# A two-layer trunk on one core: a unit's queries projected ahead of its values, and two kinds of weight tiles packed in pairs

## The chip, the cores and the metric

The kernel runs on one core of one Trainium2 chip. The metric is the device time of one execution in microseconds (us). Engines are named as in the profile: PE is TensorE's matrix multiply, PEld its weight load, DVE VectorE, ACT ScalarE, POOL GpSimd, SP SyncE, which only issues transfers. L1941 is line 1941 of the kernel before. In the changed kernel the same lines of the engines' programs stand 19 lines further down (L1941 is L1960 there, L1134 L1153, L2085 L2104).

## The reference

1,024 tokens with 16 meta tokens ahead of them (1,040 in all) pass two layers of width 1,024; each adds its result to the scaled input and normalises.

```python
# layer 0 (even): two groups of heads share one input projection
qa, ka, va, ga, qs, ks, vs, gs = split_cols(x @ w_in, EVEN_SPLITS)
# A: 4 units of differential attention with a distance bias, softmax of two maps
w = p[:, :, 0] - lam * p[:, :, 1];  ya = rms_norm(w @ va) * silu(ga)
# B: 8 heads (4 units of two) of stick-breaking attention, times silu(gs)
# layer 1 (odd): latent attention, 8 heads
cq, ckv, k_pe, g = split_cols(x @ w_in, ODD_SPLITS)
q  = rms_norm(cq, q_norm) @ w_uq      # 128 plain and 64 rotary columns per head
kv = rms_norm(ckv, kv_norm) @ w_ukv   # 128 key and 128 value columns per head
# both: concatenated, gated, one output projection, then
h = layer_norm(ALPHA * h + y, ln_g[i], ln_b[i])
```

## The kernel before

All matrices are fp32 split into a high part in fp32r and a low remainder, and each product is the sum of three (high x high, high x low, low x high). A projection step is named (kind, unit, chunk): kinds q0, k0, v0, g0 are queries, keys, values and gate of a unit of layer 0; kn, vn, qn, qr the keys, values, plain queries and rotary queries of a head of layer 1 (qr serves two heads, so it exists for even heads alone). The 1,040 token columns are cut into three chunks of 352, 344 and 344. A step of layer 0 has 8 tiles of 128 rows, times three products, so 24 matmuls (`project`, L1918 on, the matmul at L1941); kn and vn have 2 tiles (6 matmuls), qn and qr 4 (12 matmuls). Its result lands in one of two PSUM banks and is evacuated by ACT (high part) and DVE (low part).

Weights come as tiles of 128 output columns. SP loads tile n into one of two raw buffers `wraw` (L915), POOL splits it into one of two buffers `wsp` (`split_weights`, L1035; the instructions are L1032 and L1033), and PE reads it. The split of tile n has to wait for the last product with tile n - 2. Later POOL splits 17 tiles of attention output (y) for the output projection in the same buffers.

Attention runs step by step (t): scores S (L2009, one bank per chunk of keys, three banks), then DVE, ACT or both make weights of them (in B units a sigmoid on ACT, L1393, and a scan on DVE, L1723; in layer 1 an exponential and POOL's scaling, L1222), then PE transposes them in turns T (L2029, two banks), ACT and DVE copy them as high and low part into a ring of three (L1424, L1738), and PE multiplies them with the values, X (L2059). A group g is a pair of query blocks of a unit or head. Before scores of a unit of layer 0 can be made, POOL copies the chunk's queries into the other half of the partitions (`copy_queries`, L1134). The values' transposes VT (L1980) read DVE's copy of the values in A units; in B units they read differences of neighbouring rows, which POOL makes (`step_values`, L1160 to L1164, called D). After an A unit, PE sums squares for its norm with a matrix of ones (rms0, L1954).

The output projection's 8 weight tiles (WO) are copied by ACT (L1367) and their low parts made by POOL (L1076) or DVE (L1777); they take the place of the layer's input, so their work starts only behind the last gate product. Its blocks O (L2085) have 48 matmuls each; the first two are "fill": single matmuls of them may stand between attention's instructions. The fill ("p" below) is done by PE in strict order like everything else.

The order on every engine is a table made before the kernel is built: `weave` gives each step an assumed duration and what it waits for, and `Lines.run` starts on each engine, time after time, the step that can begin first; ties go by rank, scores first, projections and fill last (RANK, "SXTVp" on PE). The order of the projections among themselves is given by hand in `in_attention`. In layer 0 it is, for u < 4, `k + v + g(u) + q` with k, v, q of unit u + 1, and for u = 4 to 6 a chunk of keys, the norm, a chunk of gate, keys, gate, then `v + q`.

```python
out += k + v[:1] + norm[:2] + v[1:2] + norm[2:] + v[2:] + proj("g0", u) + q if u < A_UNITS else k[:1] + norm + g[:1] + k[1:] + g[1:] + v + q
```

## Time and profile before

| what | value |
|---|---|
| time, median of 3 runs | 1376.29 us (1375.99 to 1381.58) |
| the profiled execution's own time | 1376.59 us |
| its span | 1374.8 us, 22,469 instructions |
| PE busy | 1320.7 us, 96% of the span, 8,400 matmuls |
| DVE, ACT, POOL busy | 874.2, 546.1, 487.3 us (64, 40, 35%) |
| granted clock of PE, mean | 0.995 |
| DMA | 88.26 MB, mean 64 GB/s |

The profile is one execution. "Idle before" an instruction is time in which its engine did nothing, with the instruction that released it. PE's busy time is modelled for overlapping matmuls; the starts are measured. The granted clock is given as a share of full speed: 1.00 is the 2.4 GHz level, 0.50 the 1.2 GHz level.

### The profile page before, as it was taken

The page shows a single profiled execution, that of the slowest core. Times are in us where ns is not written, and L with a number is a line of the kernel's source. Part 1 is how long each engine was busy: PE and PEld are TensorE (multiplying, and loading weights), DVE is VectorE, ACT ScalarE, POOL GpSimd, SP SyncE. Part 2 cuts the span into 40 slices and gives each one's busy share as a digit, 9 for nine tenths or more (in the row PEclk, how much of TensorE's full clock was granted, in tenths as well). Part 3 has the DMA queues.
Part 4 walks back from the last instruction along what each step waited for, and adds up shares of the span by engine and source line. Part 5 has one row for each costly group of instructions (what it writes and reads, how often), then busy time and mean ns, then how long its engine had stood idle before and what let it go on. Part 6 is the DMA issues. An engine that isn't in the chain of part 4 may idle for free.

```text
span 1374.8 us, 22469 instructions
## 1 busy us (share of the span) xinstructions
PE 1320.7 (96%) x8400; PEld 1243.6 (90%) x8400; DVE 874.2 (64%) x1973; ACT 546.1 (40%) x1290; POOL 487.3 (35%) x465
## 2 busy tenths in 40 slices
PE   8999999999899999997999999998999999999997
PEld 7999999999799999996888999998998999989886
DVE  5675869595587847668466323554767676676455
ACT  3443545463545535355111011533444555546200
POOL 3323232223234232347333323563433233334541
PEclk9999999999999999998999999999999999999999
DMA  6000111001011011113133211222111111205242
GB/s 221 32 32 31 47 32 40 23 31 47 32 39 40 20 43 51 60 40 123 58 123 132 93 46 41 83 81 73 36 47 39 51 41 58 66 22 177 78 163 76
DMA packets 47355, 88.26 MB, mean 64 GB/s; under 512 B 4480, under 2 KB 30080, under 8 KB 47120
## 3 DMA queue, kind: packets, MB, share of 16 engines
q1 hardware_dynamic: 44800, 78.45, 17.2%
q10 hardware_dynamic: 2448, 8.39, 1.6%
q8 instruction: 67, 1.10, 0.3%
q14 instruction: 40, 0.33, 0.1%
HBM read 66.84 MB, written 19.98 MB: 63 GB/s over the span
## 4 chain that ended last, share of the span: by engine, by line
PE 51%; DVE 5%; ACT 2%; issue 2%; POOL 1%; DMA 0%; SPq 0%; DVEq 0%; ACTq 0%; POOLq 0%
PE bank L1941 20%; PE bank L2085 14%; PE bank L2009 7%; PE bank L2059 5%; PE bank L2029 4%; ACT rtmp L1342 1%; PE bank L2107 1%; PE bank L1980 1%; DVE qpe L1605 0%; DVE rtmp L1558 0%; DVE qpe L1609 0%; DVE ring L1738 0%; DVE rtmp L1557 0%; DVE pb L1723 0%; DMA woraw<-in_wo 0%
## 5 line engine op out<-in xcount | busy, mean ns | idle before, releaser
L1941 PE MATMUL bank<-big,wsp 128*128 128x344 f32 (+2 forms) x3024 | 560.4, 328 | 15.2 <-DVE qh L1614 7.2
L1941 PEld LDWEIGHTS bank<-big,wsp 128*128 128x128 f32 x3024 | 481.7, 189 | 22.0 <-DVE qh L1614 10.5
L1032 POOL TENSOR_SCALAR wsp<-wraw 128x1024 fp32r<-128x1024 f32 (+3 forms) x92 | 84.9, 923 | 538.7 <-PE bank L1941 422.3
L1738 DVE TENSOR_TENSOR ring<-bank,ring 128x256 fp32r<-128x256 f32 (+3 forms) x292 | 156.9, 553 | 85.1 <-ACT ring L1424 82.5
L1424 ACT ACTIVATE ring<-bank 128x256 fp32r<-128x256 f32 (+3 forms) x292 | 138.6, 495 | 147.1 <-PE bank L2029 106.7
L2085 PE MATMUL bank<-big,wsp 128*128 128x512 f32 x816 | 195.9, 399 | 0.0
L1033 POOL TENSOR_TENSOR wsp<-wraw,wsp 128x1024 fp32r<-128x1024 f32 (+3 forms) x92 | 184.6, 2007 | 7.7
L2059 PE MATMUL bank<-ring,vtok 128*128 128x256 f32 (+2 forms) x1276 | 183.1, 280 | 4.2 <-DVE ring L1738 2.6
L2085 PEld LDWEIGHTS bank<-big,wsp 128*128 128x128 f32 x816 | 153.5, 190 | 35.1 <-DVE big L1777 0.2
L2059 PEld LDWEIGHTS bank<-ring,vtok 128*128 128x128 f32 (+1 forms) x1276 | 171.8, 191 | 10.0 <-issue 4.0
L1941 PE MATMUL bank<-h1t,wsp 128*128 128x344 f32 (+2 forms) x1080 | 173.9, 322 | 1.4 <-DVE lraw L1595 1.4
L1941 PEld LDWEIGHTS bank<-h1t,wsp 128*128 128x128 f32 x1080 | 170.2, 188 | 3.6 <-DVE lraw L1595 1.7
L2029 PE MATMUL bank<-eye,pb 128*128 128x128 f32 (+1 forms) x892 | 134.5, 274 | 11.3 <-DVE ring L1738 6.3
L2029 PEld LDWEIGHTS bank<-eye,pb 128*128 128x128 f32 (+1 forms) x892 | 103.1, 140 | 19.2 <-DVE ring L1738 8.3
L2009 PE MATMUL bank<-kst,qst 128*128 128x264 f32 (+9 forms) x480 | 104.3, 328 | 9.2 <-POOL qst L1134 8.2
L1723 DVE TENSOR_TENSOR_SCAN pb<-tb,distt 128x144 f32<-128x144 f32 (+4 forms) x72 | 100.6, 1409 | 5.6 <-PE bank L2029 3.7
L1222 POOL TENSOR_SCALAR pb<-pb,stat 128x144 f32<-128x144 f32 (+5 forms) x96 | 57.5, 609 | 109.7 <-DVE stat L1729 68.0
L2009 PEld LDWEIGHTS bank<-kst,qst 128*128 128x128 f32 x480 | 76.1, 189 | 21.2 <-POOL qst L1134 12.4
L1414 ACT ACTIVATE pb<-bank,stat 128x144 f32<-128x144 f32 (+6 forms) x112 | 59.7, 540 | 75.8 <-DVE stat L1694 57.8
L2009 PE MATMUL bank<-kh,qh 128*128 128x144 f32 (+6 forms) x336 | 73.4, 327 | 1.2 <-ACT pb L1414 0.8
L1805 DVE SCALAR_TENSOR_TENSOR res<-xres,bank 128x512 f32<-128x512 f32 (+1 forms) x34 | 21.9, 683 | 78.3 <-PE bank L2085 46.6
L1442 ACT ACTIVATE small<-small,eps 128x1 f32<-128x1 f32 (+1 forms) x17 | 5.0, 295 | 167.0 <-DVE small L1824 167.0
(133 smaller groups left out, 1432.5 us busy)
## 6 DMA issues: line engine op xcount, KB each, us to landing
wraw<-in_w SPq DMA_DIRECT2D x47, 512.0 KB, 3.5
wraw<-y_scratch SPq DMA_DIRECT2D x17, 448.0 KB, 3.6
woraw<-in_wo SPq DMA_DIRECT2D x12, 512.0 KB, 5.5
y_scratch<-ot SPq DMA_DIRECT2D x40, 128.0 KB, 1.7
xres<-in_x SPq DMA_DIRECT2D x8, 512.0 KB, 4.7
h_scratch<-res ACTq DMA_DIRECT2D x8, 512.0 KB, 2.6
gate_scratch<-gtmp SPq DMA_DIRECT2D x8, 512.0 KB, 2.9
gate<-gate_scratch SPq DMA_DIRECT2D x8, 512.0 KB, 3.6
```

The costliest lines, as they stand in the source:

```text
L1032: pool.wait_ge(S["pool_step"], tick(nc.gpsimd.tensor_scalar(hi, raw, 1.0, 1.0, ALU.mult, ALU.mult)))
L1033: return nc.gpsimd.tensor_tensor(lo, raw, lo_hi(hi), ALU.subtract)
L1222: nc.gpsimd.tensor_scalar(p_, p_, stat[:, t % 4, 13:14], 1.0, ALU.mult, ALU.mult)\
L1414: A(weights_of(1, slice(0, 128), g, slot, c0, c0 + w), bank[S_BANK[b]][:, 0:w], ACT.Exp, bias=st_(6, 7), scale=SCALE192, accum_out=st_(8 + ...
L1424: A(R[0:rows, r % NRING, 0, 0:w], bank[T_BANK[t]][0:rows, 0:w], ACT.Copy).then_inc(S["tr_hi"], 1)
L1723: V.tensor_tensor_scan(P[:, 0:n][:, ::-1], skip[:, ::-1], distt[0:rows, k0:k0 + n][:, ::-1], 1.0, ALU.mult, ALU.max).then_inc(S["p_ready_d ...
L1738: V.tensor_tensor(R[0:rows, r % NRING, 1, 0:w], bank[T_BANK[t]][0:rows, 0:w], lo_hi(R[0:rows, r % NRING, 0, 0:w]), ALU.subtract).then_inc( ...
L1941: ins = mm(dst, wsp[:, SLOT[kind, u], a, k, :], rhs[:, b, k0 + k, c0:c0 + w], start=(k == 0 and a == 0 and b == 0), stop=last)
L2009: ins = mm(dst, l, r, start=(k == 0), stop=(k == len(prods) - 1))
L2029: ins = nc.tensor.transpose(bank[T_BANK[t]][0:wide, at:at + rows], weights_of(layer, slice(0, rows), g, slot, k0, k0 + wide), eye[0:rows, ...
L2059: ins = mm(PO[:, o0:o0 + wide], l, B["ring"][0:rows, r % NRING, part, at:at + wide], start=(k == 0 and tile == turns[0][0] and part == 0 a ...
L2085: ins = mm(out_bank(n, half)[:, :], wsp[:, SLOT["y", n], a, k, :], wok[:, c, k, 512 * half:512 * half + 512], start=(k == tiles[0] and a = ...
```

## The change

It does two things. In layer 0 the hand-written order of projections changes from unit 3 on: unit 4's first query chunk comes ahead of unit 3's gate, its two others among the gate's, and for units 5 to 7 the queries come ahead of the values (first query chunk, first value chunk, the two other query chunks, the two other value chunks). In layer 1 the weights of a head's keys and values become one tile (`kv`, 4 tiles of rows long) and the rotary and plain queries of an even head another (`qq`, 8 long; 4 for an odd head, which has no rotary part); the order of the projections is kept. So layer 1 has 16 weight tiles for heads where it had 28. A tile is free for the next but one when its last product is done. The planner makes the whole table of orders anew from this.

```diff
+def tile_of(kind, u):
+    return ("kv", u) if kind in ("kn", "vn") else ("qq", u) if kind in ("qn", "qr") else (kind, u)
+def tile_kt(kind, u):
+    return 2 * KVL_T if kind == "kv" else QL_T * (2 - u % 2) if kind == "qq" else KT_OF.get(kind, KD)
+def kt_before(kind, u):
+    return KVL_T if kind == "vn" else QL_T * (1 - u % 2) if kind == "qn" else 0
...
             g = proj("g0", u)
-            out += k + v[:1] + norm[:2] + v[1:2] + norm[2:] + v[2:] + proj("g0", u) + q if u < A_UNITS else k[:1] + norm + g[:1] + k[1:] + g[1:] + v + q
+            if u == A_UNITS - 1:
+                g = q[:1] + g[:1] + q[1:] + g[1:]
+                q = []
+            out += k + v[:1] + norm[:2] + v[1:2] + norm[2:] + v[2:] + g + q if u < A_UNITS else k[:1] + norm + g[:1] + k[1:] + g[1:] + q[:1] + v[:1] + q[1:] + v[1:]
...
-        end = ("P", *slot_of, 2) if slot_of[0] != "y" else O_STEPS[slot_of[1]]
+        end = TILE_STEPS[slot_of][-1] if slot_of[0] != "y" else O_STEPS[slot_of[1]]
...
-SLOT = {s: n % 2 for n, s in enumerate(STATIONARY)}
+SLOT = {s: n % 2 for s, n in WEIGHT_AT.items()}
...
-            if kind == "qn":
-                return wuq_n[u]
-            if kind == "qr":
-                return wuq_r[u // 2]
-            return wukv[u, 0 if kind == "kn" else 1]
+            if kind == "qq":
+                return (wuq_1 if u % 2 else wuq_0)[u // 2]
+            return wukv[u]
...
-                            pool.wait_ge(S["proj_done"], last_turn(*before) + 1)
+                            pool.wait_ge(S["proj_done"], PTURN[TILE_STEPS[before][-1]] + 1)
...
-                        ins = mm(dst, wsp[:, SLOT[kind, u], a, k, :], rhs[:, b, k0 + k, c0:c0 + w],
+                        ins = mm(dst, wsp[:, SLOT[kind, u], a, kt_before(kind, u) + k, :], rhs[:, b, k0 + k, c0:c0 + w],
```

What the planner made of it, first on POOL between the value differences and the queries of unit 5. The wsp rows are splits of weight tiles, qst the copies of the three query chunks (352, 344, 344 columns), ot the gating of an output. Before, with D of unit 5 ahead:

```order
L1162 TENSOR_TENSOR sq<-vt 128x1039
L1164 TENSOR_SCALAR vlast<-vt 64x9 x2
L1178 TENSOR_TENSOR ot<-ot,gate 128x256
L1134 TENSOR_SCALAR qst<-qst 64x2x352 x2
L1178 TENSOR_TENSOR ot<-ot,gate 128x256
L1134 TENSOR_SCALAR qst<-qst 64x2x344 x2
L1032 TENSOR_SCALAR wsp<-wraw 128x1024
L1033 TENSOR_TENSOR wsp<-wraw,wsp 128x1024
L1134 TENSOR_SCALAR qst<-qst 64x2x344 x2
```

And in the changed kernel:

```order
L1153 TENSOR_SCALAR qst<-qst 64x2x352 x2
L1153 TENSOR_SCALAR qst<-qst 64x2x344 x2
L1197 TENSOR_TENSOR ot<-ot,gate 128x256
L1051 TENSOR_SCALAR wsp<-wraw 128x1024
L1052 TENSOR_TENSOR wsp<-wraw,wsp 128x1024
L1153 TENSOR_SCALAR qst<-qst 64x2x344 x2
L1197 TENSOR_TENSOR ot<-ot,gate 128x256
L1051 TENSOR_SCALAR wsp<-wraw 128x1024
L1052 TENSOR_TENSOR wsp<-wraw,wsp 128x1024
L1179 TENSOR_SCALAR sq<-vt 128x1
L1181 TENSOR_TENSOR sq<-vt 128x1039
```

The differences (sq) now stand behind all three query copies and behind one more weight split; one split is in front of the third query copy in both.

The second place is PE from the last gate product of unit 7 (the last row of L1941, or L1960) on: L2009 are scores, L2029 transposes of weights, L2059 products with values, L2085 the fill of the output projection. Before:

```order
L1941 MATMUL bank<-big,wsp 128x344 x3
L2059 MATMUL bank<-ring,vtok 128x256 x7
L2059 MATMUL bank<-ring,vtok 128x128
L2059 MATMUL bank<-ring,vtok 128x256
L2059 MATMUL bank<-ring,vtok 128x128
L2029 MATMUL bank<-eye,pb 128x128 x9
L2059 MATMUL bank<-ring,vtok 128x256 x10
L2085 MATMUL bank<-big,wsp 128x512 x6
L2059 MATMUL bank<-ring,vtok 128x256
```

And in the changed kernel, a little behind its last gate product:

```order
L2048 MATMUL bank<-eye,pb 128x128 x2
L2104 MATMUL bank<-big,wsp 128x512
L2048 MATMUL bank<-eye,pb 128x128 x4
L2028 MATMUL bank<-kst,qst 128x344 x4
L2104 MATMUL bank<-big,wsp 128x512 x6
L2028 MATMUL bank<-kst,qst 128x456 x4
L2028 MATMUL bank<-kst,qst 128x352 x2
L2078 MATMUL bank<-ring,vtok 128x256 x7
L2078 MATMUL bank<-ring,vtok 128x128
L2078 MATMUL bank<-ring,vtok 128x256
L2078 MATMUL bank<-ring,vtok 128x128
L2104 MATMUL bank<-big,wsp 128x512
```

Fill stands between transposes and scores from early on, where before it came in one group of 6 and then, 56 transposes and products later, one of 8.

## Rows read from the trace of the kernel before

**Rows 1.** The page: busy time by engine, and the output projection's matmuls.

```profile
PE 1320.7 (96%) x8400; PEld 1243.6 (90%) x8400; DVE 874.2 (64%) x1973; ACT 546.1 (40%) x1290; POOL 487.3 (35%) x465
...
L2085 PE MATMUL bank<-big,wsp 128*128 128x512 f32 x816 | 195.9, 399 | 0.0
```

**Rows 2.** Busy time by stretch; the first line names the columns.

```profile
core 0: us, PE busy (x) PEld busy (x) DVE busy (x) ACT busy (x) POOL busy (x), PEclk, DMA share, GB/s
309.00:626.30 317.30, 306.02 (x2095) 294.10 (x2093) 212.43 (x356) 145.14 (x365) 105.61 (x89) 1.00 0.13 40
626.30:631.90 5.60, 3.28 (x22) 2.52 (x23) 3.27 (x7) 5.58 (x11) 5.43 (x4) 1.00 0.81 287
631.90:635.30 3.40, 3.40 (x14) 3.02 (x13) 3.40 (x4) 3.38 (x6) 3.32 (x3) 0.50 0.37 149
635.30:645.50 10.20, 6.06 (x42) 4.75 (x40) 9.44 (x9) 6.19 (x11) 10.20 (x4) 1.00 0.18 47
645.50:652.30 6.80, 6.04 (x23) 5.43 (x24) 6.74 (x8) 1.09 (x2) 6.80 (x3) 0.50 0.76 239
930.00:1279.00 349.00, 333.50 (x2330) 321.80 (x2329) 237.90 (x654) 173.58 (x473) 128.78 (x192) 1.00 0.19 63
```

**Rows 3.** Waits of PE in 309:626.3: us in total, times, longest.

```profile
PE bank L2009 <- POOL qst L1134: 7.5, 6, 2.7
PE bank L1954 <- ACT sq L1354: 1.2, 1, 1.2
PE bank L2059 <- DVE ot L1750: 1.2, 1, 1.2
```

**Rows 4.** Timeline of PE: start, us, instruction, [idle before <- releaser].

```profile
360.10 1.27 PE L2009 MATMUL bank<-kst,qst 128*128 128x392 f32 x6 [2.66 <-POOL qst L1134]
...
446.01 1.28 PE L2009 MATMUL bank<-kst,qst 128*128 128x392 f32 x6 [1.43 <-POOL qst L1134]
...
603.16 3.94 PE L1941 MATMUL bank<-big,wsp 128*128 128x352 f32 x23
```

**Rows 5.** Timeline of POOL ahead of the second of these waits, unit 5.

```profile
438.62 1.65 POOL L1032 TENSOR_SCALAR wsp<-wraw 128x1024 fp32r<-128x1024 f32 x1 [4.30 <-PE bank L1941]
440.35 3.09 POOL L1033 TENSOR_TENSOR wsp<-wraw,wsp 128x1024 fp32r<-128x1024 f32 x1
443.59 2.36 POOL L1134 TENSOR_SCALAR qst<-qst 64x688 fp32r<-64x688 f32 x2
```

**Rows 6.** Timeline of POOL, unit 7: a weight split, then the value differences.

```profile
583.52 1.05 POOL L1032 TENSOR_SCALAR wsp<-wraw 128x1024 fp32r<-128x1024 f32 x1 [4.66 <-PE bank L1941]
584.65 2.40 POOL L1033 TENSOR_TENSOR wsp<-wraw,wsp 128x1024 fp32r<-128x1024 f32 x1
...
587.16 1.93 POOL L1162 TENSOR_TENSOR sq<-vt 128x1039 f32<-128x1039 f32 x1
```

**Rows 7.** Timeline of ACT ahead of unit 3's first logarithm.

```profile
364.14 1.28 ACT L1354 ACT_TABLE_LOAD   x1
```

**Rows 8.** Timelines of POOL and DVE in 639:653.

```profile
639.30 15.12 POOL L1076 TENSOR_TENSOR big<-woraw,big 128x1024 fp32r<-128x1024 f32 x4
...
641.98 3.64 DVE L1723 TENSOR_TENSOR_SCAN pb<-tb,distt 128x1040 f32<-128x1040 f32 x1
...
647.46 1.39 DVE L1777 TENSOR_TENSOR big<-pre_keys,big 128x1024 fp32r<-128x1024 f32 x1
648.77 3.39 DVE L1777 TENSOR_TENSOR big<-pre_values,big 128x1024 fp32r<-128x1024 f32 x1
```

**Rows 9.** Timelines of PE and DVE at head 0 of the second layer.

```profile
946.56 4.00 PE L1941 MATMUL bank<-big,wsp 128*128 128x336 f32 x24 [1.19 <-POOL wsp L1033]
...
951.68 0.51 DVE L1614 TENSOR_TENSOR qh<-bank,qh 128x336 fp32r<-128x336 f32 x1
...
952.25 0.89 PE L1941 MATMUL bank<-big,wsp 128*128 128x344 f32 x4 [1.68 <-DVE qh L1614]
```

**Rows 10.** Waits of PE in 930:1279: us in total, times, longest.

```profile
PE bank L1941 <- DVE qh L1614: 7.2, 8, 1.7
```

More of the change, by code:

```diff
@@ L235 @@
 PROJ = [s for s in BEFORE[0] + WITHIN[0] + BEFORE[1] + WITHIN[1] if s[0] == "P"]
-TILES = [[s[1:3] for s in BEFORE[n] + WITHIN[n] if s[0] == "P" and s[1] != "rms0" and s[3] == 0] for n in range(2)]
+TILE_STEPS = {}
+for _s in PROJ:
+    if _s[1] != "rms0":
+        TILE_STEPS.setdefault(tile_of(*_s[1:3]), []).append(_s)
+TILES = [list(dict.fromkeys(tile_of(*s[1:3]) for s in BEFORE[n] + WITHIN[n] if s[0] == "P" and s[1] != "rms0"))
+         for n in range(2)]
 O_STEPS = [("O", 0, b) for b in [META_Q] + list(range(NB))] + [("O", 1, b) for b in range(NB)]
@@ L240 @@
 WEIGHT_AT = {s: n for n, s in enumerate(WEIGHTS)}
+WEIGHT_AT |= {s[1:3]: WEIGHT_AT[tile] for tile, steps in TILE_STEPS.items() for s in steps}
 STATIONARY = WEIGHTS
@@ L459, in weight @@
             L.put("sp", "L", ("LW", n), 65, ([("pool", ("V" if slot_of[0] == "y" else "W", n - 2))] if n - 2 >= first_split else []) + stored, 6500 if kind == "y" and layer else 4500)
-        kt = KT_OF.get(kind, KD)
+        kt = tile_kt(kind, u)
         L.put("pool", "W", ("W", n), 430 * kt, ([("sp", ("LW", n))] if n >= first_w + 2 else []) + done, 70)
@@ L703, in last_turn, with trunk_kernel @@
     return PTURN[("P", kind, u, len(CHUNKS) - 1)]
-def trunk_kernel(nc, ht, x, meta, w0, wo0, w1, wuq_n, wuq_r, wukv, wo1, lng, lnb, lam, subln,
+def trunk_kernel(nc, ht, x, meta, w0, wo0, w1, wuq_0, wuq_1, wukv, wo1, lng, lnb, lam, subln,
                  qnorm, kvnorm, dist, masks, rope, out):
@@ L913, in weights @@
                     else:
-                        dst, src = wraw[:, n % 2, 0:KT_OF[kind] * 128], w_src(kind, u)
+                        dst, src = wraw[:, n % 2, 0:tile_kt(kind, u) * 128], w_src(kind, u)
                     sp.dma_start(dst, src).then_inc(slot("w_raw", n), 16)
@@ L1040, in split_weights @@
                     arrived(pool, "w_raw", n)
-                    kt, i = KT_OF.get(kind, KD - 1), STATIONARY.index((kind, u))
+                    kt, i = KD - 1 if kind == "y" else tile_kt(kind, u), STATIONARY.index((kind, u))
                     if i >= 2:
@@ L2179 @@
     wuq = a["od_w_uq"][0]
-    wuq_n = np.stack([tiles(wuq[:, 192 * h_:192 * h_ + 128]) for h_ in range(HEADS)])
-    wuq_r = np.stack([tiles(np.concatenate([wuq[:, 192 * h_ + 128:192 * h_ + 192] for h_ in (2 * j, 2 * j + 1)], 1))
-                      for j in range(HEADS // 2)])
+    wuq_n = [tiles(wuq[:, 192 * h_:192 * h_ + 128]) for h_ in range(HEADS)]
+    wuq_r = [tiles(np.concatenate([wuq[:, 192 * h_ + 128:192 * h_ + 192] for h_ in (2 * j, 2 * j + 1)], 1))
+             for j in range(HEADS // 2)]
+    wuq_0 = np.stack([np.concatenate([r, n], 1) for r, n in zip(wuq_r, wuq_n[0::2])])
+    wuq_1 = np.stack(wuq_n[1::2])
     wkv = a["od_w_ukv"][0]
-    wukv = np.stack([np.stack([tiles(wkv[:, 256 * h_ + 128 * z:256 * h_ + 128 * z + 128]) for z in range(2)])
+    wukv = np.stack([np.concatenate([tiles(wkv[:, 256 * h_ + 128 * z:256 * h_ + 128 * z + 128]) for z in range(2)], 1)
                      for h_ in range(HEADS)])
@@ L2199 @@
     rope = np.stack([np.tile(cos, (4, 1)), np.tile(np.concatenate([-sin, sin], 0), (2, 1))], 1).astype(np.float32)
-    arrays = dict(ht=ht, x=a["x"][0], meta=a["meta"], w0=w0, w1=w1, wuq_n=wuq_n, wuq_r=wuq_r, wukv=wukv,
+    arrays = dict(ht=ht, x=a["x"][0], meta=a["meta"], w0=w0, w1=w1, wuq_0=wuq_0, wuq_1=wuq_1, wukv=wukv,
                   wo0=wo0, wo1=wo1, lng=a["ln_g"], lnb=a["ln_b"], lam=lam, subln=a["ev_subln"].reshape(128, 1),
```

## The prediction

> **What bounds the kernel now.** I read the engine shares first: PE is busy 1320.7 of 1374.8 us [rows 1], so this edit, which adds and drops no matmul (8,400 before; the built program of the change has the same count), can only earn idle PE time, or PE time spent at half clock. The table by stretches [rows 2] says where these lie. In 309:626.3, the first layer from the last A unit's gate to the last gate product, PE idles 11.3 us (317.3 less 306.0). In the 34.3 us behind it, the end of the first layer's attention, it idles 7.2 us, and in two of the five pieces (3.4 and 6.8 us) the granted clock is 0.50, the 1.2 GHz level, against 1.00 elsewhere; before each fall PE had stood idle for much of the piece ahead (2.3 of 5.6 us, 4.1 of 10.2 us). The second layer's attention, 930:1279, idles 15.5 us. Everything else is the same program in the same order. The waits by releaser [rows 3] then name the causes in 309:626.3: 7.5 of 11.3 us are scores (L2009) waiting for POOL's copy of queries (L1134). The timeline of PE [rows 4] shows two of the four large ones; they are 2.66, 1.43, 1.75 and 1.21 us, one in each B unit, and POOL's own timeline [rows 5] why: the split of the next weight tile (1.65 + 3.09 us) is in front of the third chunk's copy (2.36 us), and both start only when PE has ended the unit's last query product, so the copy ends 7.4 us after it. PE's score step arrives 6 us after it.
>
> **Part 1, queries one product sooner.** In B units 4 to 7 all query products now come ahead of the value products (two of three, with the first value chunk between). POOL's order keeps the split ahead of the third copy in units 5 and 6, as the first two order pieces show, so the copy still ends 7.4 us after the product. But PE now has two more value chunks (24 matmuls each; 23 take 3.9 us, 0.16 each, by [rows 4]), the next key chunk and gate matmuls behind it before it needs the copy: over 11 us. The three waits of 1.43, 1.75 and 1.21 us go, 4.4 us. In unit 4 the third copy stands behind one split as before, but PE does about 6.5 us of gate product, transposes and scores first, against 5.3 to 7.4 us: of 2.66 us I leave 0.5. The wait of 1.2 us for an output (L1750) [rows 3] goes too, since scores and query matmuls now stand between those two steps. Removed: 4.4 + 2.2 + 1.2 = 7.8 us.
>
> What it adds in the same stretch. (a) Values are late instead: the transposes of values wait for POOL's difference step D (1.93 us and two small operations, 2.6 us as I take it, [rows 6]). In unit 5 D is behind a split (1.05 + 2.40 us alone), so it ends about 6.3 us after the last value product, or 7.6 with a slow split (1.65 + 3.09); PE brings 24 + 18 matmuls, 6.7 us, and the same split is needed after 24 matmuls, 3.9 us, against 3.6 to 4.8 us. I take 0.7 us for each of units 5 and 6 and 0.2 for unit 7, 1.6 us; bounds 0 and 4. (b) The three mean products of unit 3, spread between scores before with one wait of 1.2 us (L1954) [rows 3], now stand in a row. ACT has to load a table (1.28 us) and take a logarithm each [rows 7], and the second waits for the key chunk's evacuation (about 2 us): I take 2.2 us, one more than before; bounds 0 and 3. In sum the stretch gives 7.8 - 1.6 - 1.0 = 5.2 us; bounds 1.5 and 8.
>
> **Part 1 behind the last gate product (the tail).** This is the largest unknown. The third and fourth order pieces show what moved: before, one first group of 6 output matmuls came after 29 transposes and products, now all 96 of the first two output blocks are spread through the attention that is left, which is more than before by the scores of three steps. That is 23 us of fill (195.9 us over 816, 0.24 each, [rows 1]) where 26 matmuls were. Set against it, each fill matmul waits in order for the splits of the output weights, and nothing behind it on PE may pass. Counting from the end of the last gate product: POOL splits a y tile (seven eighths of the 3.45 us of [rows 6], 3.0), gates a group, then splits the first output weight (2.4 like a tile's subtraction; [rows 8] has four in 15.12, 3.8 each, when they meet DVE), so the first fill matmul starts at 6.3 us at best. PE reaches it with 2.9 us of work, held also by the ring transposes: in front of their evacuation DVE now has a weight split (1.39 us), an output and a scan of 656 columns (1.5 us), some 4 us behind the 3.7 us that ACT and DVE need for the gate and the two ring pieces left. The bank is free at about 7.8 us, so some 5 us are idle there, about 1 more up to the third group, and 1.4 at the last two weights (POOL ends them at 24 and 28 us, PE arrives at 23.4 and 26.6). I get 7.4 us idle against 7.2. After such an idle start I expect one fall of the clock, not two: PE worked 9.4 us at half clock [rows 2], which cost half, 4.7 us; one fall a little longer than the second leaves 3.5. The tail gives 1 us. Its bounds are wide: the fill hides all waits after the first and the clock stays up (a gain of 8), or every DVE row of [rows 8] comes at its long value (a loss of 8).
>
> Here a rule of the skill bears on it. [Rows 8] show the same kind of subtraction at 1.39 and at 3.39 us on DVE, a scan of 1,040 columns at 3.64 us, and POOL's four at 3.8 us each where the split alone takes 2.40 [rows 6]. By the Trainium skill, page "SBUF — State Buffer", section "SBUF: two separate sides" (Who interferes with whom), DVE and GpSimd hold a shared port pair exclusively for an instruction and the loser blocks, so such work adds instead of overlapping. The trace agrees. The rule speaks against this edit, because more scans now fall into the same stretch as the eight splits; it is rival B below, priced there from the rows.
>
> **Part 2, packed tiles in the second layer.** 28 weight tiles become 16: 12 loads and 24 POOL instructions fewer. POOL is busy 128.8 of 349 us there [rows 2] and ends one PE wait, 1.19 us [rows 9]. At the first head that wait goes, because the plain queries' weights come with the rotary ones. What is late next is DVE: the plain chunk can only be freed behind the rotation of the first rotary chunk, and the DVE row [rows 9] ends at 952.2, where PE starts (952.25), whatever came between. So the 1.19 us is given back in the next wait, now 1.68. Against it, the packed tile of 1,024 columns must be split whole before the first rotary product, 3.45 us (4.7 with a slow split), and PE has 18 key matmuls there, 2.9 us, with their evacuation. I take +0.2, bounds -1 and +1.4. With two slots, key-value tiles now all use one and query tiles the other, so key tile 1 can be split only after the last value product of head 0 (512 columns, half of 3.45 us); PE has 2.3 us between. Later heads have 36 or more projection matmuls in between, 5.7 us, against 1.7 to 4.7 us, so nothing. The other waits on DVE's qh, 5.5 us [rows 10], come from four evacuations per query pair and are in the new order as before: head 2 now stands as head 6 did, head 6 as head 2. Zero, bounds -3 and +3.
>
> **Sum**, against the profiled execution's own time (1376.6 us, its span 1374.8): -5.2 - 1.0 + 0.2 = -6.0, so 1370.6 us. The median of the runs shown is 1376.3, 0.3 us lower, within their spread. About 0.5% (6.9 us) is what a measurement of this kernel can tell from no change: the forecast is a small gain just inside it.
>
> **A second rule.** [Rows 4] show the same wait once per unit. The Trainium skill, page "Perfetto Trace Analysis", section "Identifying Performance Opportunities", says that a gap which repeats on the engine that should be saturated can mean too few buffers. The POOL rows [rows 5] say order instead: the copy is behind a split. By the rule the waits would stay, since no buffer is added, and the sum would be -1.6; that is rival C.
>
> **Rivals.**
> A. The fill works better. The waits in the tail are covered but for the first, and PE does not fall to half clock: of 7.2 + 4.7 = 11.9 us some 3 to 4 remain. Gain 8 + 5.2, so 1363 us. For it: 96 fill matmuls, 23 us, stand in a stretch that idled 7.2. Against it: POOL needs 28 us for the weights they wait for.
> B. Slower. In the tail the first fill matmul stands in front of scores and transposes on PE while POOL and DVE block each other. Six POOL splits at 3.8 instead of 2.4 us end 8 us later, DVE's two at 3.39. PE is turned back at each weight, 8 more us idle, and the clock stays at half for them. Tail +12, less 5.2: +7, about 1383 us. It decides from the point where the fourth weight ends later than PE's arrival, about 15 us after the last gate product.
> C. The waits only move: value transposes and the k and g tiles take over what the queries lost (bound 4 us of (a), 3 of (b)), tail even: -1, about 1376 us.
> D. The packing costs more than it spares in the second layer, since an 8-tile split holds up POOL's scaling of weights (L1222) for up to 4.7 us in heads 2, 4 and 6: +3 on the forecast, 1374 us, inside its range.
>
> **How the numbers follow.** Forecast (with D) 0.52, from 1366 to 1375; A 0.23; C 0.14; B 0.11. Faster by over 0.5% (below 1369.4): A and a third of the forecast, 0.40. Slower by over 0.5% (above 1383.2): half of B and something unforeseen, 0.08. Within: 0.52. The range for 8 in 10 takes in A and C and leaves most of B: 1362 to 1379 us.
>
> **What would show it.** Right: no wait of L2009 on POOL's query copy over 0.6 us in units 5 to 7; waits of the value transposes (L1980, now L1999) on POOL or of L1941 on the split below 1 us each; three mean products in a row with about 2 us in front of them; the first output matmul some 6 to 8 us behind the last gate product; one fall of the clock; second layer's attention at 15 to 16 us idle with no wait on a split. Wrong: tail idle below 4 or above 12 us, or a second layer that differs by over 3 us.

## The result and the profile after

The changed kernel takes **1389.55 us** (median of 4 runs, 1389.17 to 1394.35) where the kernel before takes 1376.62 beside it: ratio 1.0101, 95% interval 1.0081 to 1.0122, some 13 to 14 us slower. The forecast was 1370.6 us with a range of 1362 to 1379; the result lies outside it, on the side to which rival B pointed, but not for rival B's reason.

The profiled execution of the changed kernel took 1394.35 us. It is the slowest of the four: the others took 1389.2 to 1389.8 us at mean granted clocks of 0.989 to 0.991, against its 0.985. Its parts therefore add up to more than the medians differ by. Cut at the same matmuls by their number, the two profiled executions give the following (idle is the sum of PE's gaps over 0.1 us, the last column the time at the 1.2 GHz level; both are differences, after less before):

| stage | before | after | of it PE idle | at 1.2 GHz |
|---|---|---|---|---|
| last A unit's attention and unit 4 (matmul 1856 to 2540; in after the last is behind unit 5's first scores) | 108.8 us | 118.4 | +3.9 | +12.0 |
| units 5 to 7 (to 3890, ahead of unit 7's third query chunk's scores) | 199.1 | 208.6 | +4.3 | +8.5 |
| the end of the first layer's attention (to 4292) | 82.5 | 78.8 | -0.6 | -3.4 |
| output projection, second layer's input projections (to 5742) | 251.7 | 251.7 | 0 | 0 |
| second layer's attention to the last matmul | 426.3 | 431.1 | +2.5 | +6.8 |

The first two stages lose 19.1 us, the tail gains 3.7, the second layer loses 4.8. That is 20.2 us; the spans differ by 17.7, because the changed execution was 2.5 us ahead at its hundredth matmul already. The first lines of the page, against [rows 1], hold the clock already: as many matmuls are busy 9.5 us longer.

```profile
span 1392.5 us, 22425 instructions
## 1 busy us (share of the span) xinstructions
PE 1330.2 (96%) x8400; PEld 1251.4 (90%) x8400; DVE 881.7 (63%) x1973; ACT 548.4 (39%) x1290; POOL 483.0 (35%) x441
```

The waits of PE in 309:642, by releaser (us in total, times, longest), answer to [rows 3]:

```profile
PE bank L2028 <- POOL qst L1153: 9.7, 6, 2.8
PE bank L2028 <- ACT tb L1412: 3.4, 3, 1.3
PE bank L2048 <- DVE ring L1757: 3.0, 2, 1.6
PE bank L1973 <- DVE kst L1591: 1.5, 1, 1.5
PE bank L2078 <- DVE ot L1769: 0.8, 1, 0.8
PE bank L1960 <- POOL wsp L1052: 0.7, 1, 0.7
PE bank L1999 <- DVE vtok L1667: 0.7, 2, 0.5
```

The wait for POOL's query copy, which the change was to spare, has grown from 7.5 to 9.7 us. It is not the same wait. PE's timeline at unit 4's third chunk, and at unit 5's first score step:

```profile
354.81 1.65 PE L2028 MATMUL bank<-kst,qst 128*128 128x392 f32 x4 [2.82 <-POOL qst L1153]
...
411.81 0.89 PE L2028 MATMUL bank<-kst,qst 128*128 128x16 f32 x6 [1.69 <-POOL qst L1153]
```

The columns of the score say which chunk is waited for. 392 columns of keys belong to a late query block: that is the third chunk, as in [rows 4]; of these waits only unit 4's is left (2.82 against 2.66 us). 16 columns belong to the meta queries, the very first scores of a unit, and need the first chunk. Units 5, 6 and 7 each have this new, longer wait: 1.69, 2.05 and 2.03 us. The timelines of DVE and POOL in 404:412 show what they wait for:

```profile
404.55 2.18 DVE L1742 TENSOR_TENSOR_SCAN pb<-tb,distt 128x912 f32<-128x912 f32 x1
406.66 0.53 DVE L1757 TENSOR_TENSOR ring<-bank,ring 128x384 fp32r<-128x384 f32 x1
407.11 1.04 DVE L1595 SCALAR_TENSOR_TENSOR qst<-bank,qst 64x352 fp32r<-64x352 f32 x2
408.18 0.42 DVE L1757 TENSOR_TENSOR ring<-bank,ring 128x256 fp32r<-128x256 f32 x1
408.52 2.66 DVE L1742 TENSOR_TENSOR_SCAN pb<-tb,distt 128x1040 f32<-128x1040 f32 x1
```

```profile
408.24 3.52 POOL L1153 TENSOR_SCALAR qst<-qst 64x704 fp32r<-64x704 f32 x2 [3.42 <-DVE qst L1595]
```

POOL was idle for 3.4 us before it, so nothing stands in the copy's way. But the evacuation stands behind one scan, and the copy runs beside another and takes 3.52 us. In the kernel before the same copy was made where DVE did not scan; its rows there (POOL, then PE) are 1.64 us and a wait of 0.24:

```profile
419.49 1.64 POOL L1134 TENSOR_SCALAR qst<-qst 64x704 fp32r<-64x704 f32 x2 [0.85 <-DVE qst L1576]
...
421.18 0.90 PE L2009 MATMUL bank<-kst,qst 128*128 128x16 f32 x6 [0.24 <-POOL qst L1134]
```

Behind each new wait the granted clock falls in this execution. Busy time by stretch (columns as in [rows 2]), ahead of the first fall, in it, and the two falls of units 6 and 7:

```profile
407.50:411.80 4.30, 2.62 (x19) 2.06 (x18) 4.25 (x6) 1.58 (x3) 3.43 (x2) 1.00 0.00 0
412.90:416.30 3.40, 3.40 (x16) 3.34 (x15) 0.52 (x1) 0.00 (x0) 0.00 (x0) 0.50 0.00 0
...
498.20:501.60 3.40, 3.40 (x16) 3.33 (x16) 0.00 (x0) 0.20 (x2) 0.00 (x0) 0.50 0.02 5
...
583.60:587.00 3.40, 3.40 (x16) 3.28 (x15) 0.86 (x1) 0.00 (x0) 0.00 (x0) 0.50 0.00 0
```

A PE that is busy for 3.4 us at the 1.2 GHz level does the work of 1.7. With the falls at 317 (6.8 us), at 355 (3.4) and in the tail (6.8), the first layer has 27 us at half clock in the profiled execution behind 300 us, against 10.2 in that of before. That is more than in the other three executions, whose mean clock is higher.

### The profile page after: what moved, and what is told of

Same layout as the page of the kernel before. It is cut to its first block, busy times and chain, and to the rows that moved or that the text cites. A ratio compares the mean times of both kernels' runs of the same rounds, so it can differ in the third digit from the quotient of the medians.

```text
span 1392.5 us, 22425 instructions
## 1 busy us (share of the span) xinstructions
PE 1330.2 (96%) x8400; PEld 1251.4 (90%) x8400; DVE 881.7 (63%) x1973; ACT 548.4 (39%) x1290; POOL 483.0 (35%) x441
## 3 DMA queue, kind: packets, MB, share of 16 engines
q1 hardware_dynamic: 43072, 78.45, 17.2%
## 4 chain that ended last, share of the span: by engine, by line
PE 78%; DVE 10%; ACT 4%; issue 3%; POOL 3%; DMA 1%; SPq 0%; DVEq 0%; ACTq 0%; POOLq 0%
PE bank L1960 37%; PE bank L2104 13%; PE bank L2028 11%; PE bank L2078 9%; PE bank L2048 6%; POOL qst L1153 2%; DVE pb L1742 2%; ACT rtmp L1361 1%; PE bank L1999 1%; DVE ring L1757 1%; DMA wraw<-in_w 1%; DVE qst L1595 1%; DVE pb L1731 1%; ACT qst L1337 1%; PE bank L2126 1%
## 5 line engine op out<-in xcount | busy, mean ns | idle before, releaser
L1960 PE MATMUL bank<-big,wsp 128*128 128x344 f32 (+2 forms) x3024 | 567.5, 330 | 15.5 <-DVE qh L1633 9.1
L1960 PEld LDWEIGHTS bank<-big,wsp 128*128 128x128 f32 x3024 | 484.9, 190 | 23.4 <-DVE qh L1633 12.2
L1051 POOL TENSOR_SCALAR wsp<-wraw 128x1024 fp32r<-128x1024 f32 (+2 forms) x80 | 81.4, 1017 | 485.3 <-PE bank L1960 371.8
L1757 DVE TENSOR_TENSOR ring<-bank,ring 128x256 fp32r<-128x256 f32 (+3 forms) x292 | 156.5, 553 | 78.9 <-ACT ring L1443 76.1
L2104 PE MATMUL bank<-big,wsp 128*128 128x512 f32 x816 | 199.2, 399 | 0.0
L1052 POOL TENSOR_TENSOR wsp<-wraw,wsp 128x1024 fp32r<-128x1024 f32 (+2 forms) x80 | 179.9, 2249 | 6.7
L1960 PE MATMUL bank<-h1t,wsp 128*128 128x344 f32 (+2 forms) x1080 | 173.9, 322 | 1.4 <-DVE lraw L1614 1.4
L1960 PEld LDWEIGHTS bank<-h1t,wsp 128*128 128x128 f32 x1080 | 170.2, 188 | 3.6 <-DVE lraw L1614 1.7
L2028 PE MATMUL bank<-kst,qst 128*128 128x264 f32 (+9 forms) x480 | 112.4, 338 | 14.6 <-POOL qst L1153 10.3
L2028 PEld LDWEIGHTS bank<-kst,qst 128*128 128x128 f32 x480 | 80.9, 198 | 26.6 <-POOL qst L1153 14.4
L1153 POOL TENSOR_SCALAR qst<-qst 64x688 fp32r<-64x688 f32 (+1 forms) x48 | 45.6, 950 | 87.9 <-DVE qst L1595 84.8
```

The costliest lines, as they stand in the source:

```text
L1051: pool.wait_ge(S["pool_step"], tick(nc.gpsimd.tensor_scalar(hi, raw, 1.0, 1.0, ALU.mult, ALU.mult)))
L1052: return nc.gpsimd.tensor_tensor(lo, raw, lo_hi(hi), ALU.subtract)
L1153: ins = nc.gpsimd.tensor_scalar(to, lo_hi(from_), 1.0, 1.0, ALU.mult, ALU.mult)
L1757: V.tensor_tensor(R[0:rows, r % NRING, 1, 0:w], bank[T_BANK[t]][0:rows, 0:w], lo_hi(R[0:rows, r % NRING, 0, 0:w]), ALU.subtract).then_inc( ...
L1960: ins = mm(dst, wsp[:, SLOT[kind, u], a, kt_before(kind, u) + k, :], rhs[:, b, k0 + k, c0:c0 + w], start=(k == 0 and a == 0 and b == 0), s ...
L2028: ins = mm(dst, l, r, start=(k == 0), stop=(k == len(prods) - 1))
```

## Experiments

Each ran beside the kernel before on the same chip; ratios are to it, with their 95% intervals. Where microseconds are given from a ratio, they are the ratio's distance from 1 times 1376.3. The changed kernel's own ratio makes +13.9 us.

| run | median, us | ratio to before |
|---|---|---|
| e1 packing alone | 1380.08 | 1.0029 (1.0019 to 1.0039) |
| e2 order alone | 1386.30 | 1.0073 (1.0057 to 1.0089) |
| e3 unit 4's part of the order | 1380.62 | 1.0027 (1.0016 to 1.0039) |
| e4 units 5 to 7's part | 1384.11 | 1.0054 (1.0041 to 1.0066) |
| e5 changed, 141 idle matmuls | 1401.98 | 1.0183 (1.0169 to 1.0198) |
| e10 changed, 47 idle matmuls | 1384.85 | 1.0053 (1.0036 to 1.0070) |
| e6 changed, first scores later | 1381.28 | 1.0042 (1.0026 to 1.0058) |
| e13 changed, scan held | 1387.14 | 1.0074 (1.0059 to 1.0089) |
| e8 two kinds of queries packed alone | 1379.08 | 1.0017 (1.0008 to 1.0026) |
| e9 packing, scores first at head 5 | 1380.63 | 1.0020 (1.0008 to 1.0032) |
| e7 before, copy ahead of split | 1374.44 | 0.9988 (0.9978 to 0.9999) |
| e11 the same, units 4 to 6 | 1373.75 | 0.9966 (0.9950 to 0.9983) |
| e12 units 5 to 7, spaced | 1372.43 | 0.9963 (0.9952 to 0.9974) |

**Which part costs it: e1 to e4.** Each takes one part alone; the tiles are those of before except in e1.

```diff
 e1: the changed kernel, but
-out += k + ... + g + q if u < A_UNITS else ... + q[:1] + v[:1] + q[1:] + v[1:]
+out += k + ... + proj("g0", u) + q if u < A_UNITS else ... + v + q
 e2: the kernel before, with the changed in_attention
 e3: the kernel before, with
+            if u == A_UNITS - 1:
+                g = q[:1] + g[:1] + q[1:] + g[1:]
+                q = []
 e4: the kernel before, with
-... + v + q
+... + q[:1] + v[:1] + q[1:] + v[1:]
```

> The packed tiles of the second layer with the order of projections of before. Theory O (the order of the projections in layer 0 is what cost the time): layer 0 is as before, so only what the profile of after shows in the second layer's attention is left (one wait of 3.25 us on DVE's qh at 1155 with 6.8 us at half clock, +4.7 us to the end of the span): 1378 to 1381 us. Theory P (packing, with its 8-tile splits on POOL, is the larger part): 1384 us or more. If the second layer's difference was chance of one execution: 1376 to 1378.

> The new order of projections in layer 0 with the 28 single tiles of before. Theory O: 1384 to 1388 us, with the waits of the first scores of units 5, 6 and 7 for the first query copy (1.7 to 2.1 us each) and a fall of the granted clock to 0.50 behind each of them. Theory P: 1380 us or less.

> Only the part of the order that brings unit 4's queries in among unit 3's gate; units 5 to 7 as before, single tiles. Theory O, by places: unit 4's third query chunk is waited for as long as before (2.8 against 2.7 us), three gaps of 0.7 to 0.9 us and one fall of the clock (6.8 us) at 310 to 324 are new: +3 to +5 us, 1380 to 1382. Theory T (what costs is the tail behind the last gate product, where fill is spread): no change, 1376 to 1377, as the tail has units 5 to 7 in front of it.

> Only the part of the order that brings the queries of units 5 to 7 ahead of their values; unit 4 as before, single tiles. Theory O, by places: three waits of 1.4, 1.8 and 1.2 us go, three of 1.7, 2.1 and 2.0 us and two of 1.3 us come, and three falls of the clock of 3.4 us each (1.7 us lost each) are new: 4.4 out, 5.8 + 2.6 + 5.1 in, +7 to +9 us, 1383 to 1386. Theory T: the same time, but the difference lies behind the last gate product.

By the ratios packing is worth +4.0 us, the order +10.0, together 14.0 of 13.9. The order is +3.7 for unit 4 and +7.4 for units 5 to 7, 11.1 of the 10.0. So theory O holds, with packing a real second part, and theories P and T fall. The places are those of the changed kernel: e4 has the waits of 1.69, 2.06 and 2.04 us at the first scores and no other large wait for queries behind unit 4; e3 has the 2.83 us at unit 4, and its last three units are as before. In every profile with the order of units 5 to 7 and no added matmuls the tail (matmul 3890 to 4292) is 3.6 to 3.7 us shorter than before.

**What the clock costs: e5 and e10.** Idle matmuls on PE, between the wait for the score's bank and the wait for the copy.

```diff
+                for _ in range(WARM.get(t, 0)):
+                    mm(bank[S_BANK[b]][:, 0:344], big[:, 0, 0, 0:128], big[:, 0, 0, 0:344], start=True, stop=True)
                 pe.wait_ge(S["q_copied"], ...)
```

> The changed kernel with idle matmuls on PE (344 columns, into the score's own bank, overwritten by the score): 9, 11 and 11 ahead of the first scores of units 5, 6 and 7 and 16 ahead of unit 4's third query chunk, between the wait for the bank and the wait for the copy. They are 0.16 us each and fill 1.5, 1.8, 1.8 and 2.6 of the 1.7, 2.1, 2.0 and 2.8 us waited. Theory K (half of the loss is the clock that falls after such a wait): the waits end when they did, the four falls of 3.4 us at 0.50 behind them do not come, 4 x 1.7 = 6.8 us less than the changed kernel: 1382 to 1384 us. Theory W (the waiting alone costs, the clock would fall anyway, or the time is not PE's): 1388 to 1391 us.

e5 was 12 us slower than the changed kernel. Its table was by chunk, and three query blocks of a chunk come to this place: 141 idle matmuls ran (24.3 us in the profile), 94 of them with no wait to fill.

> As e5, mended: e5 put its idle matmuls ahead of every query block of those chunks, 141 in place of the 47 meant; here 47 stand at the four waits alone. Theory K (the clock that falls behind a wait is half of the loss): 6.8 us less than the changed kernel, 1382 to 1384. Theory W: 1388 to 1391. Taking 94 x 0.16 = 15.4 us from e5's 1402.0 leaves 1386.6, which lies between: then only about half of the falls are spared.

Measured: 1384.85 us, 4.7 us less by the medians, 6.6 by the ratios, for 47 matmuls (8.1 us) whose result nobody reads. Unit 5's stretch has neither the wait nor the fall, and the tail's fall is the only one left in the first layer behind 300 us:

```profile
408.00:412.00 4.00, 4.00 (x30) 3.98 (x30) 1.98 (x3) 0.35 (x2) 0.00 (x0) 1.00 0.01 4
412.00:416.00 4.00, 4.00 (x28) 4.00 (x27) 3.24 (x3) 1.52 (x4) 0.00 (x0) 1.00 0.00 0
...
631.40:638.20 6.80, 4.64 (x16) 4.10 (x17) 6.74 (x7) 4.10 (x8) 6.72 (x4) 0.50 0.26 71
```

Theory K stands at its place: a third to a half of the whole loss is the clock that falls behind waits, not the waits. The time came out just above the 1382 to 1384 us expected. That also the fall at 317 us is gone, ahead of which nothing was added, shows that a fall does not come in every execution.

The record holds the mean granted clock of every execution, not of the profiled one alone, and it bears this out. One less the clock, times the time, is the most that half clock can have cost. It is 15.3 us for the changed kernel (mean of its 4 executions), 9.1 for e10 (5), and 9.1 to 10.9 for the kernel before in the four groups beside the experiments. The rest of the time is 1375.4, 1375.9, and 1366.7 to 1367.7 us. So e10 took away clock time alone, some 6 us of it, and at least some 8 us of the changed kernel's loss are not the clock.

In the tail half clock cost nothing. e1 and e9 have the 402 matmuls of the tail in the same order as before, with 3.4 and 6.8 us at half clock in place of 10.2, and the same length to 0.2 us; PE idles the longer (11.5 us in e1 against 8.8), mostly for DVE's ring pieces. The tail by stretch, before and in e1:

```profile
606.63:689.14 82.51, 73.60 (x405) 63.39 (x403) 53.14 (x74) 32.41 (x65) 42.41 (x28) 0.94 0.25 81
```

```profile
607.13:689.47 82.34, 70.84 (x404) 61.01 (x403) 53.90 (x74) 32.33 (x65) 42.42 (x28) 0.98 0.25 81
```

Ahead of unit 5, where the same four profiles also have one order, it does cost: matmul 1856 to 2540 take 108.8 us before with none at half clock, 109.9 and 110.2 with 3.4 us of it (e8, e9) and 110.6 with 6.8 (e1).

**Why the copy is late: e6 and e13.** e6 lets the copy be and moves its reader; e13 lets the reader be and takes away what runs beside the copy.

```diff
 e6, planner, scores: the changed kernel with
+            if kind == "B" and u > A_UNITS and cq == 0:
+                after += [("pe", ("P", "q0", u, 1))]
 e13, DVE, scans of steps 51, 69 and 87: the changed kernel with
+                    if t in HELD:
+                        dve.wait_ge(S["q_copied"], Q_COPY["P", "q0", HELD[t], 0])
```

> The changed kernel, but the planner may start the first scores of units 5 to 7 only behind the second query product (as they stood before). The first query copy then has 24 more matmuls, 4 us, in front of it. Theory O (the new waits are those scores put too close behind their copy): the three waits of 1.7 to 2.1 us and their three falls of the clock go, 5.8 + 5.1 = 10.9 us less than the changed kernel: 1378 to 1381. Theory M (the waits only move: scores that come 4 us later make ACT's sigmoids, scans and transposes late): 1386 to 1390, with new waits for ring or tb.

> The changed kernel; on DVE the scan of 1,040 columns that stands behind the first query chunk's evacuation of units 5, 6 and 7 waits for POOL's copy of that chunk. Nothing else moves. Theory X (POOL's copy takes 3.5 us where it took 1.64 because DVE scans beside it, and that is the whole wait): the copy takes 1.6 to 1.7 us, the first scores start 1.7 to 2 us sooner, the three waits and their falls of the clock go, and the scans come 1.7 us later, which PE may see at the next transposes: 1379 to 1384 us. Theory O alone (the copy is late for another reason, its length is its own): copies stay at 3.5 us, waits stay, 1390 to 1394.

e6 took 8.1 us off by the ratios (8.3 by the medians). The copy is as slow as in the changed kernel, ends at 408.5, and PE comes to the scores four microseconds later without a wait. POOL and PE:

```profile
404.97 3.52 POOL L1155 TENSOR_SCALAR qst<-qst 64x704 fp32r<-64x704 f32 x2 [3.42 <-DVE qst L1597]
...
412.46 0.79 PE L2030 MATMUL bank<-kst,qst 128*128 128x16 f32 x6
```

That is at the upper end of theory O's range. Theory M falls: at ring or tb one small wait is new, 0.76 us for the ring at 607.5, beside those that the changed kernel has (1.3 us twice and 0.9).

e13 shows what makes the copy slow. With the scan held back it takes 1.63 us in all three units, the scan itself 2.33, and PE has no wait at the first scores. POOL, DVE and PE at unit 5:

```profile
409.16 1.63 POOL L1156 TENSOR_SCALAR qst<-qst 64x704 fp32r<-64x704 f32 x2 [3.42 <-DVE qst L1598]
...
410.92 2.33 DVE L1747 TENSOR_TENSOR_SCAN pb<-tb,distt 128x1040 f32<-128x1040 f32 x1 [1.40 <-POOL qst L1156]
...
410.88 0.85 PE L2033 MATMUL bank<-kst,qst 128*128 128x16 f32 x6
...
413.50 0.45 PE L2033 MATMUL bank<-kst,qst 128*128 128x144 f32 x2 [0.52 <-ACT tb L1415]
```

The copy is two instructions of 0.77 us. In the changed kernel only one of them is slow, the one that meets a running scan. POOL's second one in unit 5, and in unit 6 the scan with POOL's copy, and the copy's second instruction by itself:

```profile
409.09 2.66 POOL L1153 TENSOR_SCALAR qst<-qst 64x704 fp32r<-64x704 f32 x1
...
493.78 2.31 DVE L1742 TENSOR_TENSOR_SCAN pb<-tb,distt 128x1040 f32<-128x1040 f32 x1
493.95 3.57 POOL L1153 TENSOR_SCALAR qst<-qst 64x704 fp32r<-64x704 f32 x2 [3.82 <-DVE qst L1595]
...
496.74 0.77 POOL L1153 TENSOR_SCALAR qst<-qst 64x704 fp32r<-64x704 f32 x1
```

In all three units the slow instruction ends 0.57 us behind the scan. In unit 5, where POOL was first, the scan took 2.66 us; in units 6 and 7, where it was first itself, 2.31, as if alone. Side by side copy and scan take 3.5 us in unit 5, one after the other 1.63 + 2.33 = 4.0, so they hardly overlap, and the 1.9 us by which the copy grew are the wait. This is the rule that the prediction named for the tail (the Trainium skill, page "SBUF — State Buffer", section "SBUF: two separate sides"), that DVE and GpSimd lock each other out of a shared port pair; the trace agrees, 1.63 against 3.52 us. The time was not what theory X gave: 1387.14 us, 3.7 us less than the changed kernel by the ratios (2.4 by the medians, and the intervals overlap a little) where 6 to 10 were expected. In place of the three waits PE waits for tb, 0.5, 0.8 and 0.8 us, and the falls at 318 and 356 us are still there. A wait of 1.3 us for the ring in the tail at 647.6 is new too, but the tail as a whole is as long as in the changed kernel (78.9 against 78.8 us). The mechanism of the slow copy is shown; holding the scan pays for part of it elsewhere.

**The packing: e8 and e9.** In the second layer the changed kernel and e1 have one large new wait of 3.25 us, at head 5's second key product. PE and DVE of the changed kernel, and the granted clock there:

```profile
1155.04 1.23 PE L1960 MATMUL bank<-big,wsp 128*128 128x344 f32 x3 [3.25 <-DVE qh L1633]
```

```profile
1149.92 0.52 DVE L1575 TENSOR_TENSOR rtmp<-bank,ropet 128x344 f32<-128x344 f32 x1 [1.29 <-ACT rtmp L1361]
...
1151.74 1.63 DVE L1624 CAST qpe<-rtmp 64x344 fp32r<-64x344 f32 x2
1153.40 1.03 DVE L1628 TENSOR_TENSOR qpe<-rtmp,qpe 64x344 fp32r<-64x344 f32 x2
1154.46 0.52 DVE L1633 TENSOR_TENSOR qh<-bank,qh 128x344 fp32r<-128x344 f32 x1
```

```profile
1153.60:1160.40 6.80, 5.36 (x17) 5.26 (x18) 3.21 (x7) 0.00 (x0) 0.94 (x2) 0.50 0.73 246
```

DVE rotates head 4's third rotary chunk, 5 us, and only then frees the bank of the plain chunk. In the kernel before, the same chain stood there, with the planner's three score steps (15 matmuls) among the last plain and key products: waits of 0.73 and 0.52 us. With packed tiles the planner took other durations and other due times for the splits, put those scores elsewhere, and only 18 projection matmuls stood in front of the wait.

```diff
 e8: e1, but tiles of keys and values as before
-    return ("kv", u) if kind in ("kn", "vn") else ("qq", u) if kind in ("qn", "qr") else (kind, u)
+    return ("qq", u) if kind in ("qn", "qr") else (kind, u)
 e9: e1, and in the planner
+            if s[1:] == ("kn", 5, 1):
+                before = before + [("pe", ("S", 146, 0, 0))]
```

> The kernel before with rotary and plain queries packed as one tile, keys and values not. The planner's order of PE stays that of before but for some 30 rows. Theory R (what packing costs is the order that the planner makes of the packed keys and values, with one wait of 3.25 us on DVE's qh at head 5 and its fall of the clock): 1376 to 1378 us and no such wait. Theory Q (the split of an 8-tile, 3.5 to 4.7 us on POOL, costs it): 1380 us.

> The packed tiles alone (as in e1), but the planner may start the second key product of head 5 only behind the score step before the last of its head 4 block (three score steps, 15 matmuls of some 0.15 us, 2.3 us, that were ready there). Theory R (the 3.25 us wait for the rotation of the third rotary chunk, with nothing but 18 matmuls in front of it, and the clock that falls behind it cost what packing costs): the wait shrinks to about 1 us and the fall of 6.8 us does not come, 2.3 + 3.4 = 5.7 us at most less than e1's 1380.1: 1375 to 1378. Theory M (the wait moves on): 1379 to 1381.

e8 nearly keeps the order and has no such wait, as theory R says, but at +2.3 us (1.0017), between the two theories, it isn't free; its profile shows no row for this beside the kernel before's (the waits for DVE's qh there are 7.2 us in eight, as in [rows 10]). e9 missed: the scores that I took for ready need the third query chunk too. The wait moved onto them and grew, and theory M is nearer:

```profile
1142.79 1.32 PE L2027 MATMUL bank<-kh,qh 128*128 128x392 f32 x3 [3.88 <-DVE kh L1630]
```

What the packing's 4.0 us are made of is thus settled in part: the new wait and its fall stand in the changed kernel, e1 and e6, and e8 without them costs less, though the intervals of e1 and e8 overlap. A price of the wait by itself wasn't measured.

**A better order: e7, e11, e12.** The three take the diagnosis of [rows 4, 5] (the copy stands behind a split) by POOL's order alone, and then join it with what e6 showed.

```diff
 e7, planner, weight(n): the kernel before with
+        if slot_of[0] == "q0" and slot_of[1] >= A_UNITS:
+            done += [("pool", ("P", "q0", slot_of[1], 2))]
 e11: the same with
+        if slot_of[0] == "q0" and A_UNITS <= slot_of[1] < UNITS - 1:
 e12: e4, with e6's rule for scores, and e7's for unit 4 alone
```

> The kernel before, with one rule more in its planner: from unit 4 on, the split of the weight tile that takes the queries' slot stands behind the copy of the third query chunk on POOL. Theory S (the once-per-unit wait is the copy standing behind a split): the waits of 2.7, 1.4, 1.8 and 1.2 us go but for 0.5 us each, and the split ends some 2 us later with 24 key matmuls and attention in front of its first use: 5 to 6 us less than before, 1371 to 1373. Rival: the gate product waits for the split in its place: 1375 to 1378.

> As e7 (the kernel before, the copy of the third query chunk ahead of the split on POOL), but for units 4 to 6 alone, so that every engine's order behind unit 7's queries is that of before. In e7 the waits of units 6 and 7 were gone and those of units 4 and 5 1.2 us, but the tail idled 9.4 us in four waits where before has 6.0, with 17 us at half clock against 10.2. Theory: the tail is as before, and the waits save 1.5 + 0.3 + 1.7 us: 1372 to 1374. Rival (the tail's waits depend on when each engine arrives, not on the order): as e7, 1374 to 1376.

> The kernel before (single tiles) with the queries of units 5 to 7 ahead of their values as in e4, their first scores only behind the second query product as in e6, and unit 4's third copy ahead of the split as in e7. By the sum of the parts: e4's 1384.1, less the 8.3 us that e6 took from the changed kernel, less 1.5: 1374 to 1376, with the sigmoid waits (0.9, 1.3 and 1.3 us) and the tail of the changed kernel (4.8 us in one wait) left. If parts do not add: 1377 to 1380.

e7 missed its 1371 to 1373 us. The four waits of 2.66, 1.43, 1.75 and 1.21 us became 1.17, 1.15, 0 and 0, but the tail got longer, 84.3 us against 82.5: its own waits, by releaser, in 610:660 of e7, and its two stretches at half clock:

```profile
PE bank L2031 <- DVE ring L1740: 5.3, 3, 3.4
PE bank L2087 <- POOL big L1078: 2.8, 1, 2.8
PE bank L2061 <- DVE ring L1740: 1.8, 1, 1.8
```

```profile
628.00:638.20 10.20, 7.39 (x30) 6.33 (x30) 6.45 (x8) 5.63 (x10) 10.20 (x5) 0.50 0.26 82
...
645.10:651.90 6.80, 4.49 (x17) 4.00 (x18) 5.91 (x7) 1.09 (x2) 5.50 (x2) 0.50 0.49 169
```

e11 leaves unit 7 alone and keeps the tail of before: 0.9966, 4.7 us faster, as its theory said. The waits of 1.2 us that are left at units 4 and 5 have the scan in them: the third chunk's copies there take 3.31 and 2.43 us in e11, with scans beside them, where 1.60 is the time of one that meets none. The same holds for the copies of before, 2.92, 2.36, 2.37 and 2.28 us in units 4 to 7, so the split ahead of them was only part of those four waits. e12 is the fastest by its ratio, 0.9963 (0.9952 to 0.9974), 5.1 us faster than before and better than its expected 1374 to 1376 us, with the changed kernel's idea in it: queries ahead of values in units 5 to 7, but the scores no sooner than they were. Its page begins

```profile
span 1370.6 us, 22474 instructions
## 1 busy us (share of the span) xinstructions
PE 1317.4 (96%) x8400; PEld 1239.4 (90%) x8400; DVE 878.9 (64%) x1973; ACT 548.4 (40%) x1290; POOL 485.6 (35%) x465
```

and its one fall between 300 and 1360 us is the tail's. e11 and e12 can't be told apart. The rule of the Trainium skill, page "Perfetto Trace Analysis", section "Identifying Performance Opportunities", that a repeating gap can mean too few buffers, is not what happened here: in e7 and e11 no buffer was added and the gap went or shrank.

## Why the prediction was wrong

Step by step, as the prediction put it.

- **"The three waits of 1.43, 1.75 and 1.21 us go, 4.4 us": right.** No third chunk is waited for in units 5 to 7.
- **The step that failed is what Part 1 adds ("What it adds in the same stretch").** It listed late values (a) and the three means (b), and nothing for the first chunk. The order pieces that I read were POOL's and the tail's. On PE the planner, for which a score that can begin comes first, moved unit 5's first scores forward with the chunk, to 17 value matmuls behind it; I took them to stand where they stood. Three waits of 1.69, 2.05 and 2.03 us, 5.8 us, took the place of the 4.4, and units 5 to 7 came out 7.4 us slower (e4), not faster. e6 shows that this place alone is worth 8 with its falls of the clock. The bounds given for the stretch, a gain of 1.5 to 8 us, don't follow quite from their terms either, which give 2.0 to 9.0; no choice of (a) and (b) reaches a loss.
- **The clock had no term outside the tail, where it costs, and one in the tail, where it doesn't.** I priced waits at their length. Each new one had 3.4 us at 0.50 behind it in the profiled execution; filling four waits gave 4.7 to 6.6 us (e10). In the tail I priced half clock at 4.7 us before and 3.5 after; by e1 and e9 it is worth 0.2 at most there.
- **"Of 2.66 us I leave 0.5" (unit 4): wrong, 2.82.** I had the copy end 5.3 to 7.4 us behind the product. It ended 11.2 us behind it (343.6 to 354.8): the evacuation stood behind a scan of 2.71 us and the copy took 4.51 us in two, against 2.36 in [rows 5], with scans beside it. "The wait of 1.2 us for an output goes" was wrong too: 0.75 us of it stayed, and 0.71 and 0.89 came beside it, and 1.42 us for a transpose bank.
- **(a) values late, 1.6 us: too high,** 0.7 us for values in two waits, and no split was waited for in units 5 to 7. **(b) "2.2 us, one more than before": near,** 1.52 us. The scores' waits for ACT's tb, 3.4 us in three, were in no term.
- **The tail: right in kind, by another way.** "One fall of the clock, not two" is what came, 6.8 us in place of 3.4 and 6.8, with 4.75 us in one wait, but e1 and e9 have one fall as well with the order of before, so the number of falls is not the edit's doing. The stage gave 3.7 us; 1.2 of them are unit 7's query wait, counted above, so 2.5 against the 1 predicted. Since the 1 was made of the clock's 1.2 and that is worth nothing, the sign is luck; where the 2.5 come from was not tested. Rival B's place was wrong, but its mechanism was right: POOL and DVE block each other, and it cost time at the query copies. At the tail's splits it was less than before: POOL's six of output weights take 17.2 us in all (2.37, 2.36, 3.87, 2.39, and 6.20 for two) where they took 19.9.
- **Part 2, "+0.2, bounds -1 and +1.4; zero for the later heads, -3 and +3": too low.** The 1.19 us at head 0 fell to 0.46, and was not given back in the next wait, "now 1.68": that one is 1.11, with 0.58 new between them. "In the new order as before" failed for the later heads: 3.25 us at head 5, where I had compared the list of projections and not the scores between them. Measured +4.0 us (e1), at the end of the summed bounds (4.4).

The sum is thus: predicted -6.0; measured +3.7 for unit 4's part, +7.4 for units 5 to 7, +4.0 for packing. The parts' ratios add up to 15.1 where the whole is 13.9, within their intervals. The two errors behind it are the same one twice: the rows of before price an operation at the place where it stood, and the table that the planner makes anew moves more than the edit says.

## What to carry to other kernels

When a planner or scheduler makes the order, look up the first consumer of whatever is produced earlier: it moves forward as well, and its slack is then the planner's assumed duration against the real one, here 1.4 us against 1.6 alone and 3.5 beside a scan. Price an operation by the slowest row of its kind beside the work that it will meet, and a wait on TensorE by its length plus what the clock loses behind it, but only where TensorE sets the pace: in the tail, where it waits for others anyway, half clock cost nothing. A small rule at the one place that waits (e11, e12) beat a new global order.

## What the runs showed of the hardware

- POOL's copy of 64x704 in two instructions takes 1.63 us alone and 3.52 to 3.57 us beside a scan of 1,040 columns on DVE, in all three units; in e13 it is back at 1.63. One of the two instructions takes it all, 2.66 to 2.72 us in place of 0.77. The scan loses 0.33 us where POOL was first, and nothing where it was first itself.
- The granted clock fell behind waits of 1.69, 2.05 and 2.03 us with 3.4 us at 0.50 each in the profiled execution of the changed kernel, and so it did in e2's. In e4, with the same three waits, it fell once, for 6.8 us, behind the second. In the execution of before that is shown it did not fall at the 2.66 us, nor at the 1.75, but it did at the same 2.66 in e1, e4, e8 and e9 and at the same 1.75 in e1. So one execution does not tell whether a given wait costs a fall, and stages of two profiles that differ by 1.7 us may differ by that alone.
- Half clock costs time only where PE sets the pace: 3.4 us of it cost 1.1 to 1.4 us ahead of unit 5, and 6.8 us less of it gave nothing in the tail.
- Idle matmuls whose result is overwritten made the kernel faster, by 4.7 us for 47 of them, and 94 more in places without a wait cost 17 us.
